# Norm statistics as columns: one token to a partition, with the inverse spread by TensorE

## The reference

```python
def rms_norm(x, g):
    y = xf * lax.rsqrt(jnp.mean(xf * xf, axis=-1, keepdims=True) + EPS)
    return (y * g.astype(jnp.float32)).astype(x.dtype)

# first model, layer l (h: 512 tokens; hc: 256 context tokens, in layer 0 only behind its attention)
u = modulate(rms_norm(h, g_norm1[l]), mod[:, :, 0], mod[:, :, 1])
h = h + mod[:, :, 2] * merge_branches(u, (ya, yb, yw), ...)
u2 = modulate(rms_norm(h, g_norm2[l]), mod[:, :, 3], mod[:, :, 4])
h = h + mod[:, :, 5] * conv_ffn(u2, ...)
...
return rms_norm(h, g_final)
# second model, layer l
h = rmsnorm(x, attn_norm_w[l]); proj = h @ w_in[l]; ...
x = x + concatenate([y_ssd, y_sc, y_nsa]) @ w_out[l]
h = rmsnorm(x, ffn_norm_w[l]); ...; x = x + (silu(gate) * val) @ ffn_w_down[l]
# and at the end
return rmsnorm(x, final_norm_w)
```

## Time and profile before

| | us |
|---|---|
| median of 3 runs (3975.26 to 3977.81) | 3975.33 |
| the profiled execution's own time | 3972.31 |
| its span in the profile | 3970.2 |
| TensorE busy (share of the span) | 3839.5 (97%) |
| VectorE busy | 2232.9 (56%) |
| ScalarE busy | 1540.6 (39%) |
| POOL busy | 319.7 (8%) |

### The profile page before, as it was taken

The page is one execution under the profiler, slowest core; times in us unless marked ns, Lnnn a source line. Parts: engine busy times, 40 slices in busy tenths (PEclk is TensorE's granted clock), DMA queues, the critical chain, the costliest instruction groups (busy, mean ns, idle before and its releaser), DMA issues. The chain is left out here.

```text
span 3970.2 us, 53080 instructions
## 1 busy us (share of the span) xinstructions
PE 3839.5 (97%) x20276; PEld 3030.8 (76%) x20276; DVE 2232.9 (56%) x3890; ACT 1540.6 (39%) x2617; POOL 319.7 (8%) x282
## 2 busy tenths in 40 slices
PE   7999999999999999999999999999899999999998
PEld 5876567778888888875788788876578887667887
DVE  5355678754553543365734556276657626666752
ACT  3245661113431322255722344253544415354431
POOL 0100001111000001100000100114010010400001
PEclk9999999999999999999999999999999999999999
DMA  5210015551221121200022233322023323202332
GB/s 192 84 38 26 1 52 184 200 180 58 64 69 56 63 73 57 70 25 26 17 95 79 85 97 100 100 92 80 19 89 98 96 91 98 75 28 89 95 103 82
DMA packets 81206, 320.10 MB, mean 81 GB/s; under 512 B 9728, under 2 KB 9856, under 8 KB 80128
## 3 DMA queue, kind: packets, MB, share of 16 engines
q1 hardware_dynamic: 68064, 270.49, 21.0%
q0 software_dynamic: 12960, 47.19, 3.5%
HBM read 311.09 MB, written 2.10 MB: 79 GB/s over the span
## 5 line engine op out<-in xcount | busy, mean ns | idle before, releaser
L529 DVE TENSOR_TENSOR split_low<-weight_ring,split_high 128x1024 fp32r<-128x1024 f32 (+2 forms) x408 | 555.2, 1361 | 510.3 <-ACT split_high L521 510.1
L521 ACT ACTIVATE split_high<-weight_ring 128x1024 fp32r<-128x1024 f32 (+2 forms) x412 | 466.4, 1133 | 871.5 <-PE banks L1587 338.7
L1787 PE MATMUL banks<-normed_high,split_high 128*128 128x512 f32 x1040 | 405.6, 390 | 3.0 <-DVE normed_low L1730 2.2
L1787 PE MATMUL banks<-normed_low,split_high 128*128 128x512 f32 x1040 | 404.7, 389 | 0.0
L1787 PE MATMUL banks<-normed_high,split_low 128*128 128x512 f32 x1040 | 404.7, 389 | 0.0
L2085 PE MATMUL banks<-normed_high,split_high 128*128 128x512 f32 (+1 forms) x704 | 238.7, 339 | 2.1 <-DVE normed_low L2000 2.1
L2085 PE MATMUL banks<-normed_low,split_high 128*128 128x512 f32 (+1 forms) x704 | 237.6, 337 | 0.0
L2085 PE MATMUL banks<-normed_high,split_low 128*128 128x512 f32 (+1 forms) x704 | 237.1, 337 | 0.0
L1787 PEld LDWEIGHTS banks<-normed_high,split_high 128*128 128x128 f32 x1040 | 195.2, 188 | 47.3 <-DVE normed_low L1730 3.0
L1787 PEld LDWEIGHTS banks<-normed_high,split_low 128*128 128x128 f32 x1040 | 195.2, 188 | 40.7
L1787 PEld LDWEIGHTS banks<-normed_low,split_high 128*128 128x128 f32 x1040 | 195.2, 188 | 40.0
(11 more groups left out here) (391 smaller groups left out, 8483.7 us busy)
## 6 DMA issues: line engine op xcount, KB each, us to landing
weight_ring<-in_up SPq DMA_DIRECT2D x174, 512.0 KB, 3.5
weight_ring<-in_down SPq DMA_DIRECT2D x64, 704.0 KB, 4.1
modulation_ring<-in_ada POOLq DMA_DIRECT2D x80, 512.0 KB, 4.1
weight_ring<-in_merge SPq DMA_DIRECT2D x48, 768.0 KB, 4.4
weight_ring<-in_inputs SPq DMA_DIRECT2D x36, 512.0 KB, 3.4
weight_ring<-in_out SPq DMA_DIRECT2D x32, 512.0 KB, 3.5
weight_ring<-in_xbc SPq DMA_DIRECT2D x16, 512.0 KB, 3.5
weight_ring<-in_short SPq DMA_DIRECT2D x12, 512.0 KB, 3.5
```

Of the source, the lines that this page charges most:

```text
L521: act.activation(k.splits[0][:, (n0 + panel) % RING, 0:width], k.slot(n0 + panel)[:, 0:width], ACT.Copy).then_inc(k.high_ready.sem, 1)
L529: dve.tensor_tensor(k.splits[1][:, s, 0:width], k.ring[:, s, 0:width], k.splits[0][:, s, 0:width].bitcast(F32), ALU.subtract).then_inc(k.l ...
L1787: last = pe.matmul(sums(r, half), w, x, start=(c + j == 0), stop=(c == KT - 1 and j == 2))
```

## The change

`sum_columns` makes the squares the stationary operand and a single column of ones the moving one, so the sum of token t stands in partition t: a block of 128 tokens gives one PSUM column, and 512 tokens give 4, 768 give 6. `root_of_columns` and `invert_columns` take root and reciprocal of these columns into a small tile, `deviations`. `spread_inverse` has TensorE multiply, for each block, the column read 128 times over (stationary, 128x128) by the identity, which puts the inverse of the block's tokens into every partition of a PSUM bank. Where the scaling is done chunk by chunk (A to D, I), VectorE reads the inverse from PSUM; in E to H ScalarE copies it to SBUF, now between the fourth and the fifth chunk of its highs, where before the root stood behind the eighth. The root now stands before the first chunk. `keep_busy` is cut and put before and behind the spread. In B the second reciprocal goes, and in E the one in the middle of the convolutions. The branch of `norm` that squares and sums by itself is removed. The norms inside the attention (latents, heads) are not touched.

```diff
+def sum_columns(k, pe, bank, squared, count, start, stop):
+    for t in range(count):
+        last = pe.matmul(k.psum[:, bank, t:t + 1], squared[:, t * P:(t + 1) * P], k.table("ones")[:, 0:1],
+                         start=start and t == 0, stop=stop and t == count - 1)
+    return last
+
+def root_of_columns(k, act, bank, count, epsilon=12, at=0):
+    act.activation(k.deviations[:, at:at + count], k.psum[:, bank, 0:count], ACT.Sqrt,
+                   bias=k.scalars[:, epsilon:epsilon + 1], scale=1.0 / D).then_inc(k.deviation_ready.sem, 1)
+
+def invert_columns(k, dve, count, roots=1):
+    dve.wait_ge(*k.deviation_ready(roots))
+    dve.reciprocal(k.deviations[:, 0:count], k.deviations[:, 0:count]).then_inc(k.inverse_ready.sem, 1)
+
+def spread_inverse(k, pe, ready, targets):
+    pe.wait_ge(*ready)
+    for bank, first, count in targets:
+        for t in range(count):
+            last = pe.matmul(k.psum[:, bank, t * P:(t + 1) * P],
+                             k.deviations[:, first + t:first + t + 1].to_broadcast([P, P]), k.table("ident"),
+                             start=True, stop=True)
+        last.then_inc(k.inverse_spread.sem, 1)
...
 # norm (D and I)
-                    act.activation(k.probs[:, 2, a:b], k.psum[:, sums(g, s), 0:b - a], ACT.Sqrt,
-                                   bias=k.scalars[:, epsilon:epsilon + 1], scale=1.0 / dims[g]).then_inc(
-                                       k.deviation_ready.sem, 1)
+        root_of_columns(k, act, SQUARES_BANK, (b - a) // P)
...
-                    dve.reciprocal(k.probs[:, 3, a:b], k.probs[:, 2, a:b]).then_inc(k.inverse_ready.sem, 1)
...
+        invert_columns(k, dve, (b - a) // P)
+        dve.wait_ge(*k.inverse_spread(1))
+            dve.scalar_tensor_tensor(dst[:, a:b], src[:, a:b], gain(which), k.psum[:, SQUARES_BANK, 0:b - a],
+                                     ALU.mult, ALU.mult).then_inc(k.scaled_ready.sem, 1)
...
 # project_inputs (A and C), TensorE
-                for s, (a, b) in enumerate(columns):
-                    last = pe.matmul(k.psum[:, s, 0:b - a], k.table("ones"), k.probs[:, n % 2, a:b], start=(n == 0),
-                                     stop=(n == KT - 1))
-                last.then_inc(k.squares_summed.sem, 1)
+                sum_columns(k, pe, 0, k.probs[:, n % 2, :], T // P, n == 0, n == KT - 1).then_inc(k.squares_summed.sem, 1)
             if ada:
                 modulate()
-            keep_busy(k, pe, 12 if ada else 18)
+            keep_busy(k, pe, 2 if ada else 3)
+            spread_inverse(k, pe, k.inverse_ready(1), ((0, CTX // P, LAT // P), (1, 0, CTX // P)))
+            keep_busy(k, pe, 4 if ada else 6)
...
 # add_product (in front of D to I) and both_streams (in front of C), TensorE: each ones matmul of a region
-                pe.matmul(k.psum[:, plain_bank + region, 0:b - a], k.table("ones"), squared_tiles[:, 2, a:b], start=True,
-                          stop=False)
+            sum_columns(k, pe, plain_bank, squared_tiles[:, 2, :], blocks, True, False)
...
 # split_unscaled (E to H)
+        root_of_columns(k, act, SQUARES_BANK, LAT // P, epsilon)
+        if other is not None:
+            root_of_columns(k, act, SQUARES_BANK + 1, LAT // P, at=LAT // P)
         for c in range(KT):
             act.activation(highs[:, c, :], x[:, c, :], ACT.Copy, scale=gain[:, c:c + 1]).then_inc(
                 k.rounded_ready.sem, 1)
             if c == 3:
                 split_high(k, act, first, 1, width, None)
-        act.activation(inverse, k.psum[:, SQUARES_BANK, 0:LAT], ACT.Sqrt, bias=k.scalars[:, epsilon:epsilon + 1],
-                       scale=1.0 / D).then_inc(k.deviation_ready.sem, 1)
+                for n, target in enumerate((inverse, other)[0:spreads]):
+                    act.wait_ge(*k.inverse_spread(n + 1))
+                    act.activation(target, k.psum[:, SQUARES_BANK + n, 0:LAT], ACT.Copy).then_inc(
+                        k.inverse_copied.sem, 1)
...
         split_low(k, dve, first, 0, width, k.high_ready(1))
+        invert_columns(k, dve, spreads * LAT // P, spreads)
...
 # ffn_up (D, and F and H with late), TensorE
-        keep_busy(k, pe, 16 if late is None else 6)
+        keep_busy(k, pe, 3)
+        spread_inverse(k, pe, k.inverse_ready(0), ((SQUARES_BANK, 0, n // P),))
+        keep_busy(k, pe, 5 if late is None else 3)
...
 # norm_streams and both_streams (B), VectorE and TensorE
             if c == 0:
-                dve.wait_ge(*k.deviation_ready(s + 1))
-                if s:
-                    low_part(q - 1)
-                dve.reciprocal(k.probs[:, 3, a:b], k.probs[:, 2, a:b]).then_inc(k.inverse_ready.sem, 1)
+                dve.wait_ge(*k.inverse_spread(s + 1))
-        keep_busy(k, pe, 15)
+        keep_busy(k, pe, 3)
+        spread_inverse(k, pe, k.inverse_ready(1), ((SQUARES_BANK, CTX // P, LAT // P), (SQUARES_BANK + 1, 0, CTX // P)))
+        keep_busy(k, pe, 5)
...
 # second_branches (E and G): TensorE, POOL, VectorE
-            keep_busy(k, pe, 7)
+            keep_busy(k, pe, 2)
+            spread_inverse(k, pe, k.inverse_ready(0), [(SQUARES_BANK + n, n * LAT // P, LAT // P)
+                                                       for n in range(1 if l else 2)])
+            keep_busy(k, pe, 3)
-                pool.wait_ge(*k.root_ready(2))
+                pool.wait_ge(*k.inverse_copied(0))
-            dve.wait_ge(*k.deviation_ready(0))
-            dve.reciprocal(inverse, inverse).then_inc(k.inverse_ready.sem, 1)
-                if l == 0 and m == 5:
-                    dve.wait_ge(*k.root_ready(1))
-                    dve.reciprocal(k.probs[:, 1, 0:LAT], k.probs[:, 0, 0:LAT]).then_inc(k.root_ready.sem, 1)
...
 # last_norm (I), TensorE: no fillers
+        spread_inverse(k, pe, k.inverse_ready(0), ((SQUARES_BANK, 0, LAT // P),))
```

More of the change, by code:

```diff
@@ L475, in stream_norm, with norm, _, low_part @@
-def stream_norm(k, l, which, target, ranges, split=None, columns=(0, T), summed=False, ahead=0, block=None):
+def norm(k, group, ranges, split=None, modulation=None, ahead=0, block=None):
+    a, b, which = ranges
+    shifted = group[0][3] is not None
+    @block.gpsimd
+    def _(pool):
+        subtract_ahead(k, pool, min(ahead, 1))
+    @block.scalar
+    def _(act):
+        root_of_columns(k, act, SQUARES_BANK, (b - a) // P)
+        split_ahead(k, act, ahead)
+        for q, (src, dst, gain, shift) in enumerate(group if split else ()):
+            act.wait_ge(*k.scaled_ready(q + 1))
+            if shifted:
+                rounded = act.activation(split[0][q], dst, ACT.Identity, bias=shift(which))
+            else:
+                rounded = act.activation(split[0][q], dst, ACT.Copy)
+            rounded.then_inc(k.high_ready.sem, 1)
+    @block.vector
+    def _(dve):
+        def low_part(q):
+            dst, shift = group[q][1], group[q][3]
+            dve.wait_ge(*k.high_ready(ahead + q + 1))
+            high = split[0][q].bitcast(F32)
+            if shifted:
+                rest = dve.scalar_tensor_tensor(split[1][q], dst, shift(which), high, ALU.add, ALU.subtract)
+            else:
+                rest = dve.tensor_tensor(split[1][q], dst, high, ALU.subtract)
+            rest.then_inc(k.normed_ready.sem, 1)
+        if modulation:
+            modulated_gains(k, dve, *modulation)
+        invert_columns(k, dve, (b - a) // P)
+        dve.wait_ge(*k.inverse_spread(1))
+        if modulation:
+            dve.wait_ge(*k.gains_ready(1))
+        for q, (src, dst, gain, _) in enumerate(group):
+            dve.scalar_tensor_tensor(dst[:, a:b], src[:, a:b], gain(which), k.psum[:, SQUARES_BANK, 0:b - a],
+                                     ALU.mult, ALU.mult).then_inc(k.scaled_ready.sem, 1)
+            if ahead == 2 and q == 0:
+                dve.wait_ge(*k.low_ready(1))
+                split_low(k, dve, k.next_panel, 1, KT * P, k.high_ready(2))
+            if split and q:
+                low_part(q - 1)
+        if split:
+            low_part(len(group) - 1)
+    k.ends(deviation_ready=1, inverse_ready=1, inverse_spread=1, scaled_ready=len(group),
+           high_ready=len(group) if split else 0, normed_ready=len(group) if split else 0, gains_ready=1 if modulation else 0)
@@ L477, in stream_norm @@
+def stream_norm(k, l, which, target, ranges, split=None, columns=(0, T), ahead=0, block=None):
     a, b = columns
@@ L1537, in add_product @@
     n = end - first
-    squared_columns = [(a - first, b - first) for (a, b), _, _ in regions]
     squared_tiles = k.probs
@@ L1705, in add_product, with split_unscaled @@
            weighted_added=0 if gains is None else tiles - 2)
-def split_unscaled(k, block, gain, highs, lows, inverse, epsilon=12, inverted=True):
+def split_unscaled(k, block, gain, highs, lows, inverse, epsilon=12, other=None):
     first, width = k.next_panel, KT * P
-    x = k.stream[:, :, CTX:T]
+    x, spreads = k.stream[:, :, CTX:T], 1 if other is None else 2
     @block.scalar
@@ L2159, in _ @@
```

(3 more changed lines are left out.)

200 lines of the change are left out of this document (42 added, 158 removed).

## The result

The changed kernel is slightly slower: 3983.09 us (median of 19 runs, 3980.62 to 3986.68) against 3976.49 (19 runs, 3973.01 to 3977.81), a ratio of 1.0018 with a 95% interval of 1.0011 to 1.0025. I had forecast 3964.7. The profiled execution took 3982.84 us (span 3980.7) against 3972.31 (span 3970.2): +10.5 where the sum of my terms was -10.6.

A forecast was written before the change was run, and what follows sets the result against it. TensorE, busy 97% of the span, was taken as the bound, with gains only where it waits or plays fillers. Terms summed to -10.6 us: 3961.7 for the profiled execution, 3964.7 for the median; range 3958.5 to 3972.

The forecast's parts named there:

- A: First norm, at 22 us: the reciprocals go but the modulation path stays; -0.35 us.
- E: Second model's projection norm at 2596 us: first wait absorbs the delay, second wait (2.0) shrinks; -1.8 us.
- C: Norm at 1539 us: the reciprocal is the longest link, scaling starts at 1545.2 instead of 1548.03; -2.8 us.
- Prices: Assumed costs of new operations: 0.11 us a one-column pass, 0.17 the small reciprocal, 0.25 the small Sqrt.
- The sums, counted as zero: One-column passes replace the wide sums at the norms within 0.1 us either way, so counted as zero.
- The clock: Granted clock: G's loss of 1.7 us comes back, but one new fall (+1.7) cancels it.
- G: Second model's projection norm at 3278 us: VectorE's chain gains a little, the 1.80 wait shrinks to 0.5; -0.45 us.
- B and D: Norms at 970 and 2225 us: POOL's split_low limits when VectorE's split starts; -3.1 and -1.05 us.
- F, H, I: Feed-forward norms at 2912 and 3592 us, low part 5 later, +0.65 each; end norm at 3955, reciprocal unhidden, -2.35.
- The clock takes it back: Rival, chance 0.20: four more clock falls, at A, D, F and H, cost +6.8 us, giving 3971.5.
- Dear passes: Rival, chance 0.08: weight loads do not overlap, a pass costs 0.38 us; +44 us, 4009 or more.
- GpSimd: Rival, chance 0.07: in E, GpSimd's earlier scaling slows six more split_lows of VectorE; +4.3 us, 3969.

The follow-up runs named there:

- e6: Changed kernel with wide column sums (85 or 128 columns of ones) at all nine norms and 13 filler matmuls before the first sums; 3960.95 us, ratio 0.9963.
- e1: Changed kernel with each column-sum pass moving 128 or 85 columns of ones instead of one; 3971.45 us, ratio to the kernel before 0.9988.
- e5: Changed kernel with wide column sums at eight norms and the first norm in its old form; 3962.52 us, ratio 0.9967.
- e8: e5 with root and reciprocal before the first weight split in E to H, one filler before the spread, inverse copies behind the eighth chunk; 3962.44 us.
- e7: Changed kernel, one-column sums kept, with 13 filler matmuls in front of the first norm's sums; 3981.25 us, ratio 1.0016.
- e4: Kernel before with 24 more filler matmuls of 256 columns in front of its first product; 3984.06 us, ratio 1.0021.
- e3: Kernel before with its filler matmuls at 1, 64 or 128 columns and their number doubled; 3981.64 us (one run, total not used).

## Why the prediction was wrong, step by step

- **What bounds the kernel, C.** Right as a mechanism: with the clock held, C gave -2.71 to -2.74 for -2.8, scaling 2.9 us into the block. In the changed kernel the clock took all of it.
- **Prices.** The 0.11 us a pass was right at 2.4 GHz (0.112 in e6), the small reciprocal (0.17 to 0.19) and root (0.25 to 0.27) too. The Trainium skill ("TensorE: Matmul & The Clock Gate", LDWEIGHTS) prices a load by its own columns, 107 ns for 128, with no term for the moving side. The traces agree with that at 2.4 GHz: with 1 and with 85 moving columns C's passes stand 0.112 us apart. At 1.2 GHz the runs show 0.213, twice that price, and there the measurement decides.
- **The sums, counted as zero: the step that failed first.** "Within 0.1 us either way" holds at eight places. At A the 96 passes took 20.6 us for the old sums' 12.3, and the first product came 9.4 late, because they run with the clock that TensorE starts with, and the narrow passes never raise it. The bound I gave for a pass (0.065 to 0.36) contained 0.213; what I had not asked is at which level the engine would be there.
- **The clock: the second.** I wrote "I let one new fall (+1.7) cancel G's". B to I each had one, and of my signs of being wrong the clock below 1 at D, F and H came. (What I called 1.7 us of time at the lower level is the loss; around G the lower level lasted twice that, 3.4 us.) I had looked for falls in idle time and in missing fillers; at seven of the eight places it was the width of the sums (e1), and G is open. Compare D in e1, where TensorE does nothing for 1.72 us before the first product, and the clock stays:

```profile
2231.74 1.22 DVE L496 TENSOR_TENSOR split_low<-weight_ring,split_high 128x1024 fp32r<-128x1024 f32 x1 [0.44 <-POOL split_low L496]
...
2234.39 0.47 PE L1742 MATMUL banks<-normed_high,split_high 128*128 128x512 f32 x1 [1.72 <-issue]
```

- **B and D, clamped by POOL.** Right: the split above starts 0.03 us behind POOL's end (2229.35 + 2.36), D gave -1.10 for -1.05, and B's first product -1.2 for -1.25. B's whole is -3.64 for -3.1, but before's own fall at 992 to 1000 (1.7 us) is gone in that. Without it -1.9 would be left, so the second gain there was nearer 0.7 than the 1.85 forecast.
- **E: half right.** The second wait (2.0 us) is gone. In e1 one is left, of 1.8:

```profile
PE banks L2465 <- DVE split_low L496: 1.8, 1, 1.8
```

  But "the first wait absorbs the delay" failed: the delay of 1.3 us at 2608 is still 1.3 at 2644. VectorE's chain moved with the products. So e1 and e5 gain 0.9 to 1.0 by 2700, not 1.8; without the late low part (e8) it is 1.9, which shows it.
- **F, H, I.** Right with the clock up: +0.55 to +0.63 for +0.65 at F and H in e1, e5 and e6, -2.32 to -2.38 for -2.35 at I. F and H cost no more even with the clock down (+0.62, +0.66), since low part 5 was late anyway. The last place, I, lost 0.8 to it: eight spread passes took 2.07 us instead of 1.16.
- **G.** -0.52 for -0.45 (e5) is luck. In e1 and e5 before's own fall (3327) is gone and another (3284, 3275) stands in its place. In e6, without either, G gives -1.85; less the 1.7 of before's fall, the step itself is an estimated -0.15.
- **The rivals.** "The clock takes it back" was the right name with the wrong cause, places and size: I had it at A, D, F and H for +6.8. What it took in after, against e1, is 0.5 at B, 2.7 at C, 0.95 at D, 1.9 at E, 0.85 at I, and at A, against e6, 10.5. "Dear passes" came true at A alone, by the clock and not for want of overlap. GpSimd did not collide: its scaling starts near 2627, where before's began at 2656, and from there to 2700 no split_low of VectorE took over 1.23 us.

The sum of my terms without A is -10.25; e5, which has A in its old form, shows -9.9 in the same eight places. That nearness is in part luck: E gave 1.1 less than forecast, and B got 0.5 more with before's own fall. By the medians of the same session e5 gains 13.4, more than its trace against before's short run. The changed kernel's profiled run is 21.1 us from the forecast: 9.7 at A, 6.8 over B to I, and 4.6 in stretches that nobody changed. By the medians (+6.6 for -10.6) it is 17.2, which the 16.5 of the nine places nearly fill: the two steps above, and 1.0 at E that would have been missing with the clock up too.

## What to carry to other kernels

Ask of every replaced TensorE instruction not only how long it takes but at which clock it runs and what the clock does behind it. Here fp32 passes with 1, 64, 85 and 128 moving columns stood 0.11 to 0.12 us apart alike, so widening the sums with columns that nobody reads was free and worth 11.6 us. Where TensorE is idle before its first work, let it play fillers first: with the widened sums, 10 to 13 matmuls of 256 columns brought the first product over 9 us forward; with one-column sums (e7) it was 1.7. And place each stage against its unchanged neighbours: in a 4000 us program, stretches that nobody touched differed by up to 1.9 us between two profiled runs (e4), and the profiled run of the kernel before was 4.2 us under its median. One trace on each side is not enough for steps of this size.

## What the runs showed of the hardware

- One-column fp32 passes 0.11 us apart: the granted clock went to 0.50 at C in e3 with TensorE busy 4.00 of 4 us, to the lower level behind 24 of them at F and H (stretches of 0.75 and 0.58), and to 0.50 from 28 us on in e7. Passes of 64 and 128 columns at the same spacing kept 1.00 over 7 us (e3), and so did 96 passes of 85 columns over 10.85 us (e6).
- The same 85-column passes, begun at 1.2 GHz, did not bring the clock up in 20.8 us (e1); 26 filler passes of 256 columns did within 8 us (e6). Why 85 columns hold a level that they don't reach was not tried.
- The weight load of such a pass (fp32, 128x128) took 190 to 192 ns at 2.4 GHz (e6) and 333 at 1.2 (after, e1).
- The granted-clock column shows 1.00 from the start of the program although TensorE is at 1.2 GHz: passes 0.213 us apart read 1.00 there in the changed kernel, and 0.54 and 0.50 in e7, where a change of level had been recorded before.
- Stretches of attention that no edit touched differed by -1.6 to +1.9 us between the profiled runs of before and of before delayed by 8.5 us (e4). The delayed kernel's runs spread over 8 us, those of before over 4.8.
